# Two feed-forward layers on one core: the first block by the standard algorithm between the transposes, and three high/low buffers in the output projection

## The reference, cut

```python
def swiglu_ffn(h, w_in, w_out):
    gate, up = jnp.split(h @ w_in, 2, axis=-1)
    return (jax.nn.silu(gate) * up) @ w_out

f = swiglu_ffn(rms_norm(x, ffn1_pre_g[l]), ffn1_w_in[l], ffn1_w_out[l])
x = x + 0.5 * rms_norm(f, ffn1_post_g[l])
m = token_mixer(rms_norm(x, mix_pre_g[l]), w_mix_in[l], ...)
x = x + rms_norm(m, mix_post_g[l])
f = swiglu_ffn(rms_norm(x, ffn2_pre_g[l]), ffn2_w_in[l], ffn2_w_out[l])
x = x + 0.5 * rms_norm(f, ffn2_post_g[l])
```

## Time and profile before

| | us |
|---|---|
| median of 3 runs | 2509.0 |
| lowest, highest | 2507.47, 2509.99 |
| the profiled execution: its own time | 2505.09 |
| its span (first to last instruction) | 2503.0 |
| its mean granted TensorE clock | 0.982 |

### The profile page before, as it was taken

One profiled execution on the slowest core, in us unless ns is written; L12 is line 12 of the kernel. 1 busy time (PEld: TensorE's weight loads), 2 busy tenths in 40 slices (PEclk: granted clock), 3 DMA queues, 4 the chain that ended last, 5 costly groups with the idle time before them and its releaser, 6 DMA issues. The chain is left out here.

```text
span 2503.0 us, 31056 instructions
## 1 busy us (share of the span) xinstructions
PE 2398.2 (96%) x11203; PEld 2001.9 (80%) x11203; DVE 1494.1 (60%) x1717; ACT 822.4 (33%) x1191; POOL 1042.5 (42%) x644
## 2 busy tenths in 40 slices
PE   5999999999999999999999999999799999999997
PEld 4788888788878888888888887887578888878875
DVE  6655555446453695785785767534765555544564
ACT  4333333223454224324224232411433333322322
POOL 5445445345552223223313234322744544534464
PEclk9999999999999999999999999999799999999998
DMA  4222322335622123022022144423323322324453
GB/s 138 76 75 84 92 75 75 110 142 183 229 100 64 29 68 93 26 77 85 26 94 68 51 160 160 168 91 102 109 68 89 87 75 76 100 76 151 175 206 115
DMA packets 215699, 254.76 MB, mean 102 GB/s; under 512 B 8789, under 2 KB 161843, under 8 KB 215603
## 3 DMA queue, kind: packets, MB, share of 16 engines
q1 hardware_dynamic: 209075, 240.93, 30.0%
q10 hardware_dynamic: 6528, 12.58, 1.3%
HBM read 197.90 MB, written 55.57 MB: 101 GB/s over the span
## 5 line engine op out<-in xcount | busy, mean ns | idle before, releaser
L579 PE MATMUL PU<-XH,w_h 128*128 128x512 f32 x1008 | 400.8, 398 | 3.0 <-POOL w_l L2036 1.1
L581 PE MATMUL PU<-XH,w_l 128*128 128x512 f32 x1008 | 394.2, 391 | 0.0
L580 PE MATMUL PU<-XL,w_h 128*128 128x512 f32 x1008 | 393.9, 391 | 0.0
L2041 POOL TENSOR_TENSOR ws<-pw,ws 128x512 fp32r<-128x512 f32 x176 | 249.5, 1419 | 257.5 <-ACT ws L1115 257.5
L1683 DVE TENSOR_TENSOR hb_l<-hb_raw,hb_h 128x512 fp32r<-128x512 f32 x88 | 206.2, 2345 | 238.6 <-ACT hb_h L1194 238.6
L2085 POOL TENSOR_TENSOR wo_l<-wo_raw,wo_h 128x1024 fp32r<-128x1024 f32 x88 | 215.4, 2449 | 256.2 <-ACT wo_h L1193 256.2
L2036 POOL TENSOR_TENSOR w_l<-w_raw,w_h 128x2048 fp32r<-128x2048 f32 (+1 forms) x40 | 178.8, 4470 | 323.7 <-ACT w_h L1039 323.7
L1773 DVE SCALAR_TENSOR_TENSOR PG<-ub,cw,PG 128x512 f32<-128x512 f32 x464 | 308.0, 749 | 5.9 <-issue 5.9
L2041 POOL TENSOR_TENSOR ws<-s_sum,ws 128x512 fp32r<-128x512 f32 x132 | 174.7, 1326 | 169.6 <-ACT ws L1115 169.6
L579 PEld LDWEIGHTS PU<-XH,w_h 128*128 128x128 f32 x1008 | 190.2, 189 | 46.2 <-issue 5.5
L581 PEld LDWEIGHTS PU<-XH,w_l 128*128 128x128 f32 x1008 | 190.1, 189 | 40.3
(11 more groups left out here) (269 smaller groups left out, 5358.7 us busy)
## 6 DMA issues: line engine op xcount, KB each, us to landing
pw<-in_ffn_w_in SPq DMA_DIRECT2D x88, 512.0 KB, 5.5
wo_raw<-in_ffn_w_out SPq DMA_DIRECT2D x88, 512.0 KB, 3.4
w_raw<-in_w_mix_in SPq DMA_DIRECT2D x50, 512.0 KB, 4.6
h_d<-hid SPq DMA_DIRECT2D x44, 512.0 KB, 3.3
hb_raw<-h_d SPq DMA_DIRECT2D x88, 256.0 KB, 3.8
x_d<-FACC SPq DMA_DIRECT2D x16, 512.0 KB, 2.9
gate_d<-tmp ACTq DMA_DIRECT2D x16, 512.0 KB, 2.9
gt<-gate_d SPq DMA_DIRECT2D x16, 512.0 KB, 5.6
```

What stands on the lines that cost most here:

```text
L579: pe.matmul(dst, hi(k), xh(k), start=(n == 0), stop=False)
L580: pe.matmul(dst, hi(k), xl(k), start=False, stop=False)
L581: last = pe.matmul(dst, lo(k), xh(k), start=False, stop=(n == KT - 1))
L2041: PT(ws[:, i, 1, :, :], form_source(name, par), ws[:, i, 0, :, :], ALU.subtract).then_inc(form_lo, 1)
```

## The change

Of each feed-forward, block 0 is no longer done by the seven products but by `whole`: four sums of 24 matmuls, gate and up of each half of tokens (G00, U00, G01, U01), from the plain weight quarters A11, A12, A21, A22 and the plain x forms. B12 is a new x form for it, so that there are eight. Block 1 keeps the seven products. `FRONT_P` puts the four sums and the seven products between the eight sets of transposes: B11, B21, G00, P1, U00, P2, B12, B22, G01, T1, U01, T2, P5, T3, P6, T4, P3, P7, P4. Block 0 needs no `sums`; those of block 1 stand behind `t1_sum` now. POOL's `t3_sum` waits for the transposes of B12. Block 0's results leave from `sb1` and `u3` by two half stores. ACT's and POOL's forms before the transposes are six instead of four, and one more at the end goes.

The x forms have the same addresses in both feed-forwards, and `pw` lies at 48 KB, over a buffer of the mixer. Hence its four loads for the second feed-forward stand behind `mm_t` 8, two of them behind `h_lo`.

In the output projection the high and low parts have three buffers (`m % 3`), the raw ones still two. A high part of step l may be written once PE has finished step l-3. In the second half's end PE does steps 19 and 20 for token tiles 0 and 1, then, tile by tile, what is left of step 19, 20 and 21.

```diff
-FRONT_W = [("A11", 0, "A11", None), ("A11", 1, "S3", None), ("A12", 0, "A12", None), ("A12", 1, "A22", None),
...
+FRONT_P = ["G00", "P1", "U00", "P2", "G01", "U01", "P5", "P6", "P3", "P7", "P4"]
+FRONT_W = [("A11", 0, "A11", None), ("A12", 0, "A12", None), ("A11", 1, "S2", None), ("A21", 0, "S3", None),
+           ("A22", 0, "A22", None), ("A12", 1, "S4", None), ("S1", 1, "S1", None), ("S2", 1, "S2", "P1"),
+           ("S4", 1, "S4", "P2"), ("S3", 1, "S3", "U01"), ("A22", 1, "A22", "U01")]
...
-        for n, homes in enumerate((
-                {"B11": 144, "T2": 160, "T1": 176, "B21": 0, "B22": 16, "T3": 32, "T4": 48},
-                {"B11": 0, "B21": 16, "B22": 32, "T3": 48, "T1": 144, "T2": 160, "T4": 176})):
-            XF.append({f: (at(f"{f}h{n}", kb, [P, 4, HALF], FR), at(f"{f}l{n}", kb + 8, [P, 4, HALF], FR))
...
+        XF = {f: (at(f"{f}h", kb, [P, 4, HALF], FR), at(f"{f}l", kb + 8, [P, 4, HALF], FR))
+              for f, kb in {"B21": 0, "B22": 16, "T3": 32, "T1": 64, "B11": 144, "T2": 160, "T4": 176}.items()}
+        XF["B12"] = (at("B12h", 176, [P, 4, HALF], FR), at("B12l", 184, [P, 4, HALF], FR))
+        pw = at("pw", 48, [P, 2, 2, KT, P])
...
-        wo_raw = [at(f"wo_raw{n}", kb, [P, 2, D]) for n, kb in enumerate((144, 0))]
-        hb_raw = [at(f"hb_raw{n}", kb, [P, 2, HALF]) for n, kb in enumerate((152, 8))]
-        hb_h = [at(f"hb_h{n}", kb, [P, 2, HALF], FR) for n, kb in enumerate((156, 12))]
...
+        wo_raw = at("wo_raw", 144, [P, 2, D])
...
+        wo_h = [at(f"wo_h{r}", kb, [P, D], FR) for r, kb in enumerate((156, 160, 164))]
+        wo_l = [at(f"wo_l{r}", kb, [P, D], FR) for r, kb in enumerate((168, 172, 176))]
+        hb_h = [at(f"hb_h{r}", kb, [P, HALF], FR) for r, kb in enumerate((2, 10, 18))]
...
                 pair_raw(n, 2, 0, wv)
-                store_hid(n, 0, 0)
+                for half, buf in enumerate((sb1, u3)):
+                    sp.wait_ge(hid_ready, N_H * n + half + 1)
+                    sp.dma_start(h_d[0, :, half * HALF:(half + 1) * HALF], buf[:, 0, :]).then_inc(hid_stored[0], 16)
...
-            for a in range(2):
-                gate_raw(a, w1v, a)
-            load_x(range(4, TT))
-            for a in range(2):
-                up_raw(a, w1v, a)
+            gate_raw(0, w1v, 0)
+            load_x(range(4, 6))
+            up_raw(0, w1v, 0)
+            gate_raw(1, w1v, 1)
+            load_x(range(6, TT))
+            up_raw(1, w1v, 1)
...
-            sp.wait_ge(w_lo, S_END)
-            for a in range(2):
-                gate_raw(a, w2v, a)
-                up_raw(a, w2v, a)
             sp.wait_ge(mm_t, 7)
             residual(1, x1_d, 0)
             sp.wait_ge(mm_t, 8)
             post_gain(1, mix_post_g)
             residual(1, x1_d, 1)
+            gate_raw(0, w2v, 0)
             pre_gain(1, ffn2_pre_g)
+            up_raw(0, w2v, 0)
             sp.wait_ge(h_lo, HU_CP + 8)
             residual(1, x1_d, 2)
+            gate_raw(1, w2v, 1)
+            up_raw(1, w2v, 1)
...
+            def whole(n, half, up):
+
+                if half:
...
+                    form, xform = (("A11", "A12"), ("A21", "A22"))[up][part], f"B{part + 1}{half + 1}"
+                    slot = SLOTS.index("S3" if form == "A21" else form)
+                    hi, lo = XF[xform]
+                    pe.wait_ge(form_lo, N_P * n + forms_done(0, form))
+                    for k in range(4):
+                        pe.wait_ge(x_lo, fills_of(n, xform) + k + 1)
+                        pe.matmul(dst, ws[:, slot, 0, k, :], hi[:, k, :], start=(part + k == 0), stop=False)
...
             def hidden_phase(n):
...
                 x_transposes(n, "B11")
                 x_transposes(n, "B21")
-                front("P1", 0)
-                front("P1", 1, False)
-                front("P2", 0)
-                front("P2", 1, False)
+                whole(n, 0, 0)
+                front("P1")
+                whole(n, 0, 1)
+                front("P2")
+                x_transposes(n, "B12")
+                x_transposes(n, "B22")
+                whole(n, 1, 0)
                 x_transposes(n, "T1")
-                x_transposes(n, "B22")
-                front("P5", 0)
+                whole(n, 1, 1)
                 x_transposes(n, "T2")
-                front("P3", 0)
+                front("P5")
                 x_transposes(n, "T3")
-                front("P6", 0)
+                front("P6")
                 x_transposes(n, "T4")
-                front("P7", 0)
-                front("P4", 0)
-                pe.wait_ge(x_lo, 28 * (n + 1))
+                front("P3")
+                front("P7")
...
-                for name in ("P6", "P5", "P7", "P3", "P4"):
-                    front(name, 1, False)
+                front("P4")
...
+                def block(m, t, c, first, final):
+                    r = m % 3
...
+                operands(0)
+                for t in (0, 2, 1, 3):
+                    pe.wait_ge(taken, N_T * (n + 1) - (7 if t in (0, 2) else 0))
+                    for c in range(2):
+                        last = block(0, t, c, True, False)
+                last.then_inc(step_done, 1)
+                steps(1, 6)
+                step(FB - 3, FB - 3)
...
+                m = 2 * FB - 3
...
-                    last.then_inc(step_done, 1)
...
-                            if between:
-                                between(t)
+                            block(k, t, c, False, False)
+                operands(m + 2)
+                for t in range(4):
+                    for c in range(2):
+                        if t >= 2:
+                            block(m, t, c, False, False)
+                            block(m + 1, t, c, False, False)
+                        block(m + 2, t, c, False, True).then_inc(o_done, 1)
+                    if between:
+                        between(t)
...
+                if form == "T4":
+                    act.wait_ge(p_done, N_P * n + products_done(0, "U01"))
...
+            def whole_gate(n, half):
+                act.wait_ge(p_done, N_P * n + products_done(0, f"G0{half}"))
+                A((sb1, u3)[half][:, 0, :], BANK["X"][0], ACT.Silu).then_inc((gated0, gated1)[half], 1)
...
+                elif l == 2:
+                    act.wait_ge(p_done, N_P * (n + 1))
+                elif l == FB + 2:
...
                 else:
-                    act.wait_ge(step_done, done + max(k - 1, 0))
-                A(wo_h[n][:, m % 2, :], wo_raw[n][:, m % 2, :], ACT.Copy).then_inc(wo_hi, 1)
-                A(hb_h[n][:, m % 2, :], hb_raw[n][:, m % 2, :], ACT.Copy).then_inc(hb_hi, 1)
+                    act.wait_ge(step_done, N_STEP * n + (l - 2 if l < FB + 2 else l - 3))
+                A(wo_h[r][:, :], wo_raw[:, m % 2, :], ACT.Copy).then_inc(wo_hi, 1)
+                A(hb_h[r][:, :], hb_raw[:, m % 2, :], ACT.Copy).then_inc(hb_hi, 1)
...
+            front_forms(0, 3, 5)
             square2(7, 0, junk_x)
-            front_forms(0, 3, 7)
+            front_forms(0, 5, 6)
 
             def front_rest(n):
-                copy_p1(n, 0, 0)
+                whole_gate(n, 0)
                 copy_p1(n, 1, 1)
-                front_forms(n, 7, 8)
+                front_forms(n, 6, 8)
+                gate0(n, 1, 1)
...
+                x_fill(n, "B22")
                 front_forms(n, 8, 9)
...
-                gate0(n, 1, 1)
+                whole_gate(n, 1)
                 x_fill(n, "T1")
-                x_fill(n, "B22")
...
                 x_fill(n, "T2")
...
                 x_fill(n, "T3")
...
-            front_forms(1, 0, 4)
+            front_forms(1, 0, 6)
...
-            front_forms(1, 4, 7)
             front_rest(1)
...
                 done_product(n, j, product)
+                if front and name == "U2":
+                    dve.wait_ge(t34_sum, 8 * (n + 1))
...
+            def whole_hidden(n, half):
+                done_product(n, 0, f"U0{half}")
+                dve.wait_ge((gated0, gated1)[half], FB * n + 1)
+                buf = (sb1, u3)[half][:, 0, :]
+                TT_(buf, BANK["Y"][0], buf, ALU.mult).then_inc(hid_ready, 1)
...
-                x_rest(n, "T2")
-                sums(n, 1, 1, 0)
-                x_rest(n, "T3")
-                take(n, 0, 0, "U2")
-                take(n, 0, 0, "U4")
-                take(n, 0, 0, "C12")
+                take(n, 1, 1, "U2")
+                take(n, 1, 1, "U4")
                 x_rest(n, "T4")
-                take(n, 0, 0, "U3")
-                take(n, 0, 0, "C22")
-                take(n, 0, 0, "C21")
-                hidden1(n, 0, 0)
-                hidden0(n, 0, 0)
+                sums(n, 2, 0, 1)
                 if n == 0:
                     constants()
-                sums(n, 2, 0, 1)
-                hidden_pair(n, 1, 1)
+                for name in ("C12", "U3", "C22", "C21"):
+                    take(n, 1, 1, name)
...
             def front_rest(n):
 
-                take(n, 0, 0, "C11")
```

(24 more changed lines are left out.)

300 lines of the change are left out of this document (154 added, 146 removed), and 4 rows, old and new, of the table FRONT_W.

## The result

The changed kernel takes 2474.6 us (2473.7 to 2477.7, 4 runs) against 2508.7 before: ratio 0.9873, 95% interval 0.9861 to 0.9886, 34 us less. Run again with the experiments it took 2471.2, ratio 0.9856 (0.9839 to 0.9872). The profiled execution has a span of 2473.7 us, 29.3 less than that of before; the two differ by less than the medians because the profiled execution of before lay 3.6 us under this comparison's median and that of the change 0.9 over it.

The account below looks back on a forecast made before the run. PE, busy 96% of the span, was taken as the bound, so gains come only where it waits. Terms -11 (first front), -19 (projections), -5.5 (junction and second front), -2.5 (tail) sum to -38: 2471 us, range 2460 to 2488.

Parts of the forecast that it names:

- First front: First feed-forward's start: PE's waits get other work in their place, loop starts at 81 instead of 92.3, -11 us.
- Port of DVE and POOL: First front: DVE instructions reading two SBUF operands share a locked port with GpSimd; 1.75 beside POOL, 0.68 alone.
- the T3 sums would hit `sums` of block 1: First front: POOL's later T3 sums slow these instead of the T1 sums, losing 1.9 us again: -9 instead of -11.
- Projections: Both output projections: high parts written a step earlier remove most low-part waits and the slow clock after, -19 us.
- the third step's wait: Output projections: two waits of 2.97 us stay, since raw buffers are still two and their loads keep their place.
- Junction: Mixer to second feed-forward: late gate loads make `post` 10 late and B11 4 to 8 late, taken as +6.
- the idle rest shrinks: Junction: of 35.7 us from `post` to B11 DVE was busy 29.7; the rest shrinks with all tiles added already.
- Second front: Second feed-forward's start: same edits as the first, its first transposes' waits shared with the late `post`, -11.5 us.
- Tail: Kernel's end: last drains follow the last matmul by about 0.7 instead of 3.2 us, -2.5.
- Half-given fronts: Rival: DVE bounds both fronts and waits return at later places; 2478 to 2489 us, chance 0.19.
- The ring brings nothing: Rival: projection waits are on loads, where two raw buffers decide, so three buffers gain nothing; 2490 us, chance 0.05.
- Slower by the late load: Rival: at the junction a gate load landing after about 1793, some 44 us after issue, makes a loss; chance 0.03.

Follow-up runs that it names:

- sums_later: Changed kernel with block 1's sums behind the low parts of B12 and B22 in both fronts, ACT's and POOL's order adapted: 2469.4 us, ratio 0.9844.
- full_again: The changed kernel without any edit, timed once more beside the first group of experiments: 2471.2 us, ratio 0.9856 to the kernel before.
- ring_only: Kernel before with only the output projection changed (three buffers of high and low parts, new order of last steps): 2483.5 us, ratio 0.9901.
- ring_old_end: Changed kernel with three buffers but the old order of the last steps, 20 and 21 together by token tile: 2476.3 us, ratio 0.9869.
- third_load_first: Changed kernel with each projection's third-step loads ahead of the last hidden block's store on SyncE's list: 2464.4 us, ratio 0.9822.
- forms_behind: Changed kernel with the second front's six forms moved behind statistics on ACT and POOL, loads still late: 2457.1 us, ratio 0.9801.

## Why the prediction was right, point by point

2471 was forecast, 2474.6 and 2471.2 were measured. By stages the misses are small and mostly of one sign: the terms add up to -38, the spans to -29.3 and -34.9. That the second measurement meets the forecast to 0.2 us is luck, helped by a mixer 3.7 us shorter than in the profile of before.

- **First front, -11 forecast, -9.2 to -10.6 measured.** The walk through PE, DVE and ACT was right to B12's first bank (free at 45.7 by the forecast; B22's transposes began at 46.13). The term that was mis-sized is what stands between there and G01: 2.5 us were left for it, and it took 3.3. The larger part of that is the clock, which the forecast put at nothing here, though it had priced it behind the wait of 4.27 us in the projections: from the wait to 51.8 it was granted at 0.50, and the same set on the heels of the same low parts took 2.21 us at 1.00 (`sums_later`), which leaves 0.5 for the low parts' pace. G01's first matmuls lost another 1.1 us in 49.46 to 52.00. In `full_again`, with 3.4 us at the lower clock instead of 6.8, the stage is 1.5 us shorter. The remainder, 32.0 with 1 to 2 in reserve, was 33.2.
- **Port of DVE and POOL.** The trace agrees with the rule quoted from the Trainium skill ("SBUF — State Buffer", "Who interferes with whom"): 1.15 us for a T1 sum beside POOL, 0.62 alone. The step "the T3 sums would hit `sums` of block 1" did not come: the one of these sums that was slow stood behind a low part of POOL, as it had before. The T3 sums ran beside `whole_hidden` and the `take` of C11, which read PSUM and SBUF and took 0.68 each. Of the 2.1 us that the T1 sums gained 1.2 came back on the T2 sums (5.79 at 51.08, 4.62 before), and PE did not wait for them.
- **Projections, -19 forecast, -17.6 and -17.5.** The mechanism held: high parts a step earlier, as `ring_only` shows without the new fronts and `ring_old_end` without the end order. The term that was missing is the clock behind the third step's wait: in the changed kernel 14 matmuls went at 0.43 us instead of 0.23 there, 2.8 us, and none did in the kernel before. What was wrong besides is the step on that wait itself. The forecast said that it stays because the raw buffers are still two, from ACT's 10.41 us of waiting on the transfer. The wait did stay, but the transfer was late since SyncE stood at the store of the last hidden block in front of it; `third_load_first` shows it with the two buffers untouched. The row named a DMA; whether its buffer or its place in the queue made it late stands in SyncE's timeline, which the forecast did not use.
- **Junction, +6 forecast, +9.5 measured.** `post` was put 10 late and was 9.8 late, by two misses that cancel: counted from the mixer's last output group as in the kernel before, the last gate load was issued at 1747.0 instead of 1748 to 1749, and was there 8.4 us later instead of 6 to 7. The step that failed is "the idle rest shrinks": the 35.7 us from `post` to B11 stayed 35.5, and DVE's idle time in it too (6.1 us before, 6.0 after). DVE, ACT and POOL hand each tile on to each other, and here a later start with more tiles ready did not shorten that chain; even with `post` 16 us earlier (`forms_behind`) it was 36.1. What paces it within was not taken apart.
- **Second front, -11.5 forecast, -10.6 and -11.4.** Close; there the wait before B22's transposes was 0.91 us only. With the junction it was to give -5.5 and gave -1.1 and -1.5.
- **Tail, -2.5 forecast, -2.0.** By the end order alone, as `ring_old_end` shows. The forecast let the drains follow the last matmul by 3.2 us before, but its own rows give 2.5 (2490.50 to 2493.00); with that its sum would have been -1.8.
- **Rivals.** Half-given fronts: no, they gave nearly whole. The ring brings nothing: no, by `ring_only`. Slower by the late load: the mechanism is real, at a price of 9.6 us with a landing of 8.4 after its issue, far from the 44 us at which the change would have been a loss.
- **The mixer** was counted at nothing and moved between 1004.5 and 1015.7 in kernels that do not differ in it. That is the clock for the most part (last section).

## What to carry to other kernels

Where several engines each run their own list, a step that waits for a late transfer holds up all that is queued behind it: put it behind the work that has its data (15 us here for one move of six forms), before trying to make the transfer itself earlier (9.6 us). When a profile says that an engine waited for a transfer, read the issuing queue before counting buffers. Price a chain of hand-overs between engines at its measured length; the idle time within it was no slack here. Where a forecast leaves PE a wait like those here (2.7 to 4.3 us), allow for a stretch at the lower clock behind it.
